# Two transformer layers at the end of a long kernel: weights awaited by halves, attention paced by one step per group, copies and stores rearranged

## The reference, cut to what matters

```
for l in range(DEPTH_2):                       # 2 layers
    proj = h @ w_in[l]                         # retention q,k,v,g; pool u; attention q,k,v; forget logits
    o_r  = silu(g_r) * head_group_norm(retention(q_r, k_r, v_r))      # 4 heads, width 384
    o_p  = multiscale_pool(u_p) * pool_scale                          # width 256
    o_f  = forgetting_attention(q_f, k_f, v_f, logf)                  # 6 heads, width 384, causal softmax
    h    = layer_norm(ALPHA * h + concat(o_r, o_p, o_f) @ w_out[l])
    h    = layer_norm(ALPHA * h + (silu(h @ w1[l]) * (h @ w3[l])) @ w2[l])    # D_FF = 2816
return h[:, 16:]
```

## Time and profile before

| | us |
|---|---|
| median of three runs | 3325.28 (3321.03 to 3330.27) |
| the profiled execution | 3315.55 |
| its span | 3313.3 |
| TensorE busy (matmul) in the span | 3153.7 (95%) |
| VectorE, ScalarE busy | 882.8, 555.3 |
| mean granted TensorE clock | 0.967 of full speed |

### The profile page before, as it was taken

The page is one execution under the profiler, slowest core; times in us unless marked ns, Lnnn a source line. Parts: engine busy times, 40 slices in busy tenths (PEclk is TensorE's granted clock), DMA queues, the critical chain, the costliest instruction groups (busy, mean ns, idle before and its releaser), DMA issues.

```text
span 3313.3 us, 52517 instructions
## 1 busy us (share of the span) xinstructions
PE 3153.7 (95%) x22815; PEld 1784.6 (54%) x22815; DVE 882.8 (27%) x1852; ACT 555.3 (17%) x1217; POOL 45.6 (1%) x58
## 2 busy tenths in 40 slices
PE   9878878999999999999989999999999999999998
PEld 3454545343434343434335667574785658675865
DVE  2633444212121211111263431323133112222101
ACT  1332310111111111111121310220112010120000
POOL 0000001000000000000010000000000000000000
PEclk9888878999999999999989999999999999999999
DMA  9800035999999999999843333323333353243531
GB/s 402 339 26 27 27 120 194 403 404 414 405 411 406 415 405 414 406 413 406 330 170 128 114 138 127 147 102 153 132 134 127 115 197 132 90 159 114 214 149 68
DMA packets 90266, 751.82 MB, mean 227 GB/s; under 512 B 9977, under 2 KB 24513, under 8 KB 50353
## 3 DMA queue, kind: packets, MB, share of 16 engines
q1 hardware_dynamic: 62080, 693.52, 52.8%
q10 hardware_dynamic: 21536, 30.51, 2.7%
q0 software_dynamic: 6544, 26.24, 2.1%
HBM read 683.10 MB, written 67.13 MB: 226 GB/s over the span
## 4 chain that ended last, share of the span: by engine, by line
PE 84%; DVE 3%; ACT 2%; DMA 1%; issue 1%; POOL 1%; ACTq 0%; POOLq 0%; DVEq 0%
PE psum L1207 20%; PE psum L1543 19%; PE psum L1284 10%; PE psum L1560 9%; PE psum L1487 5%; PE psum L1529 3%; PE psum L1498 3%; PE psum L772 3%; PE psum L1307 1%; PE psum L1160 1%; PE psum L790 1%; PE psum L1366 1%; PE psum L1404 1%; PE psum L1432 1%; PE psum L1377 1%
## 5 line engine op out<-in xcount | busy, mean ns | idle before, releaser
L1207 PE MATMUL psum<-weight_ring,arena 128*32 128x512 f32 x6192 | 691.4, 594 | 5.7 <-issue 5.4
L1543 PE MATMUL psum<-arena,weight_ring 128*128 128x256 f32 (+1 forms) x2816 | 632.7, 384 | 2.7 <-ACT arena L2169 2.7
L1543 PEld LDWEIGHTS psum<-arena,weight_ring 128*128 128x128 f32 x2816 | 528.9, 189 | 97.6 <-issue 10.4
L1207 PEld LDWEIGHTS psum<-weight_ring,arena 128*32 128x32 f32 x6192 | 197.2, 110 | 429.5 <-issue 416.7
L1284 PE MATMUL psum<-weight_ring,arena 128*32 128x256 f32 x6144 | 338.2, 380 | 1.0
L1560 PE MATMUL psum<-weight_ring 128*128 128x512 f32 x704 | 308.2, 597 | 4.2 <-DVE weight_ring L3069 4.2
L1284 PEld LDWEIGHTS psum<-weight_ring,arena 128*32 128x32 f32 x6144 | 196.6, 110 | 134.8 <-ACT arena L2049 8.6
L2807 DVE COPY arena<-psum 128x384 f32<-128x384 f32 x32 | 17.9, 559 | 802.8 <-PE psum L772 802.8
L1560 PEld LDWEIGHTS psum<-weight_ring 128*128 128x128 f32 x704 | 133.8, 191 | 171.9 <-issue 164.6
L1487 PE MATMUL psum<-weight_ring,arena 128*128 128x512 f32 (+2 forms) x512 | 171.8, 493 | 1.5 <-ACT arena L2169 1.5
L3069 DVE TENSOR_TENSOR weight_ring<-weight_ring,psum 128x256 f32<-128x256 f32 (+1 forms) x88 | 37.4, 425 | 501.8 <-PE psum L1543 498.5
(11 more groups left out here) (421 smaller groups left out, 2407.5 us busy)
## 6 DMA issues: line engine op xcount, KB each, us to landing
weight_ring<-exp_gu SPq DMA_DIRECT2D x129, 2048.0 KB, 13.3
weight_ring<-weights SPq DMA_DIRECT2D x104, 2048.0 KB, 7.8
weight_ring<-exp_down SPq DMA_DIRECT2D x64, 2048.0 KB, 12.8
x_sorted<-arena SPq DMA_DIRECT2D x2, 10752.0 KB
arena<-x_sorted ACTq DMA_DIRECT2D x33, 384.0 KB, 10.3
y_sorted<-arena ACTq DMA_DIRECT2D x128, 96.0 KB, 11.7
y_sorted<-arena SPq DMA_DIRECT2D x2, 5632.0 KB, 39.6
y_sorted<-arena SPq DMA_DIRECT2D x2, 5120.0 KB, 37.3
```

What stands on the lines that cost most here:

```text
L1207: mm = pe.matmul(psum[j * GROUP:(j + 1) * GROUP, g, :], xg[:, k, g * GROUP:(g + 1) * GROUP], w[:, kk, j * 512:(j + 1) * 512], start=(k == ...
L1543: mm = pe.matmul(bank[:, 0:b - a], w[:, k, col:col + P], h2_t[:, k, a:b], start=(k == 0), stop=(k == KT - 1))
```

## The change

- `mix` asks for the second W_OUT piece only when half 1 begins. It waits for the last softmax output only ahead of the last of the eight matmuls of the first group; before that it waits for the fourth of six units.
- The transposes of the retention rows and ScalarE's copies of them move from `mix` into attention step `turn_at = fox_at + 3`, in all four attentions. They use the ring `main` as before.
- `feed_down(1, A, 0)` takes one attention step per group, as all others do.
- Into the layers, ScalarE takes the last tile's two roots after its first and its third copy of turned rows, not ahead of all five. At the turn of (1, B) it takes the last root after its first copy.
- In `feed_down`, VectorE scales the tile before ahead of the wait for the group's matmuls, and makes the statistics of half 0 when half 0 is done.
- In layer 1 the scaled rows are written in two halves; SP, behind its last weight load, stores each half (256 KB) as it is ready. Pool stores nothing more.

The diff, without the parts that only pass arguments along:

```diff
@@ TensorE, attend @@
+                    if k == plan.turn_at:
+                        pe.wait_ge(sem("ret_ready"), run + 1)
+                        for t in rows_of(l, x):
+                            n = SIZE[t]
+                            bank = main.bank(pe)
+                            for e in range(3):
+                                mm = transpose(bank[:, e * n:(e + 1) * n], u2[0:n, t, U_QK + e * P:U_QK + (e + 1) * P], n)
+                            main.ship(mm, ("mix", l, t), "a")
@@ TensorE, mix @@
                 fox_turns.rest(pe)
-                pe.wait_ge(sem("ret_ready"), RUNS[l, x] + 1)
-                for t in rows_of(l, x):
...
-                pe.wait_ge(*job)
-                fox_outs.rest(pe)
-                ws = [weights(l, W_OUT + half) for half in range(2)]
+                pe.wait_ge(*main.drained_of(("mix", l, rows_of(l, x)[-1])))
+                pe.wait_ge(*fox_outs.drained_of(("fox", l, x, 3)))
+                ws = []
                 for half, t in rows_items(l, x):
+                    if t == WHOLE[x][0]:
+                        ws.append(weights(l, W_OUT + half))
...
                     for k in range(KT):
+                        if k == KT - 1 and (half, t) == (0, WHOLE[x][0]):
+                            fox_outs.rest(pe)
@@ all engines, layers @@
-                feed_down(1, "A", 0, steps, 2)
+                feed_down(1, "A", 0, steps)
@@ SP @@
-            sp.wait_ge(out_landed, 16 * TT)
+            for t in range(1, NT2):
+                for half in range(2):
+                    part = slice(half * 512, (half + 1) * 512)
+                    sp.wait_ge(sem("layer_start"), final_count(t, half))
+                    sp.dma_start(io["out"][(t - 1) * P:t * P, part], h2[:, t, part]).then_inc(out_landed, 16)
+            sp.wait_ge(out_landed, 16 * 2 * TT)
@@ Pool @@
-            for t in range(1, NT2):
-                pool.wait_ge(sem("layer_start"), start_count(LAYERS, t))
-                pool.dma_start(io["out"][(t - 1) * P:t * P, :], h2[:, t, :]).then_inc(out_landed, 16)
@@ ScalarE, gated_embedding @@
-                    rows_root(A, t)
-                    rows_root(A, t)
+                    if t + 1 < TT:
+                        rows_root(A, t)
+                        rows_root(A, t)
@@ ScalarE, attend: ahead of the copies and exponentials of the step @@
+                    if k == plan.turn_at:
+                        mix_rows(l, x)
@@ ScalarE, turn_rows: behind each copy @@
+                    if later:
+                        roots(later.pop(0))
@@ ScalarE, layers @@
-                project(0, "A", steps, EARLY_STEPS)
+                project(0, "A", steps, EARLY_STEPS, roots_after=(TT - 1, None, TT - 1))
-                feed_down(1, "A", 1, none)
-                turn_rows("mid", 1, "B")
+                last = feed_down(1, "A", 1, none, True)
+                turn_rows("mid", 1, "B", (last,))
@@ VectorE, norm_scaled @@
-                V.did(dve.scalar_tensor_tensor(row, row, deviation, ln_par2[0:n, 1, :], ALU.mult, ALU.add), ready)
+                for part in range(parts):
+                    cut = slice(part * D // parts, (part + 1) * D // parts)
+                    V.did(dve.scalar_tensor_tensor(row[:, cut], row[:, cut], deviation, ln_par2[0:n, 1, cut], ALU.mult, ALU.add), ready)
@@ VectorE, feed_down @@
+                centered, parts = None, 2 if l == LAYERS - 1 else 1
                 for half, t in rows_items(l, x):
-                    each(steps, n_steps)
+                    each(steps)
+                    if centered is not None:
+                        norm_scaled(centered, sem("layer_start"), parts)
+                        centered = None
                     bank = main.take(dve, ("down", l, c, half, t))
...
                     if c == 1:
-                        if centered is not None:
-                            norm_scaled(centered, sem("layer_start"))
-                            centered = None
-                        if half != 0:
-                            V.settle_other(main.drained["v"])
+                        V.settle_other(main.drained["v"])
+                        if half == 0:
+                            half_stats(t, 0)
+                        else:
                             dve.wait_ge(sem("layer_ln_landed"), 16 * landed)
                             centered = norm_centered(t)
```

More of the change, by code:

```diff
@@ L134, in __init__ @@
         self.units = [(m, u) for m in range(FH // 2) for u in range(2)]
+        self.turn_at = self.fox_at + 3
         self.steps = self.fox_at + len(self.units) + 2
@@ L688, in start_count, with final_count @@
             return t + 1 if l == 0 else NT2 + END_ORDER.index((l - 1, t)) + 1
+        def final_count(t, half):
+            return NT2 + len(END_ORDER) - len(rows_of(LAYERS - 1, "A")) - len(WHOLE["B"]) + 2 * (t - 1) + half + 1
         def project_items(x):
@@ L1545, in feed_up, with feed_down @@
                     piece_free[at] = main.done()
-            def feed_down(l, x, c, steps, n_steps=1):
+            def feed_down(l, x, c, steps):
                 a, b = span(l, x)
@@ L2170, in turn_rows, with project @@
                               main.drained["a"])
-            def project(l, x, steps=None, pace=(), items=(0, 99), mid_roots=()):
+                    if later:
+                        roots(later.pop(0))
+            def project(l, x, steps=None, pace=(), items=(0, 99), mid_roots=(), roots_after=()):
                 if items[0] == 0:
-                    turn_rows("start", l, x)
+                    turn_rows("start", l, x, roots_after)
                 roots(*mid_roots)
@@ L2214, in feed_up, with feed_down @@
                     A.did(act.activation(ff_t[:, f - FF_CHUNKS[c][0], 0:b - a], bank[:, 0:b - a], ACT.Silu), main.drained["a"])
-            def feed_down(l, x, c, steps, n_steps=1):
+            def feed_down(l, x, c, steps, leave=False):
                 last = None
                 for half, t in rows_items(l, x):
-                    each(steps, n_steps)
+                    each(steps)
                     if c == 1:
@@ L2222, in feed_down @@
                         last = t if half != 0 else None
-                if c == 1:
+                if c == 1 and not leave:
                     roots(last)
+                return last
             def feed(l, x, steps):
@@ L2247, in layers @@
                 each(steps, PLANS["B"].steps)
-                mix(0, "B")
                 roots(3)
@@ L2254, in layers @@
                 each(steps, PLANS["A"].steps)
-                mix(1, "A")
                 roots(1)
@@ L2260, in layers @@
                 feed_up(1, "A", 0, steps)
-                feed_down(1, "A", 0, steps, 2)
+                feed_down(1, "A", 0, steps)
                 feed_up(1, "A", 1, steps)
                 each(steps, PLANS["B"].steps)
-                mix(1, "B")
                 roots(3, 4)
-                feed_down(1, "A", 1, none)
-                turn_rows("mid", 1, "B")
+                last = feed_down(1, "A", 1, none, True)
+                turn_rows("mid", 1, "B", (last,))
                 feed(1, "B", none)
@@ L3069, in feed_up, with half_stats @@
                     V.did(dve.tensor_tensor(g, g, bank[:, 0:b - a], ALU.mult), main.drained["v"])
+            def half_stats(t, half):
+                n = SIZE[t]
+                V.did(dve.bn_stats(ln_stats[0:n, t, half * 6:half * 6 + 6], h2[0:n, t, half * 512:(half + 1) * 512]))
             def norm_centered(t):
@@ L3074, in norm_centered @@
                 row, stats = h2[0:n, t, :], ln_stats[0:n, t, :]
-                for half in range(2):
-                    V.did(dve.bn_stats(stats[:, half * 6:half * 6 + 6], row[:, half * 512:(half + 1) * 512]))
+                if t == 0:
+                    half_stats(t, 0)
+                half_stats(t, 1)
                 V.settle()
@@ L3142, in layers @@
                 feed_up(1, "A", 0, steps)
-                feed_down(1, "A", 0, steps, None, 2)
+                feed_down(1, "A", 0, steps)
                 feed_up(1, "A", 1, steps)
```

21 lines of the change are left out of this document (8 added, 13 removed).

## The result

The changed kernel takes 3277.66 us (median of 4 runs, 3277.50 to 3282.41), the kernel before in the same session 3324.86 us (4 runs, 3321.03 to 3330.27): ratio 0.986, interval 0.9843 to 0.9877. The gain is 47.2 us at the medians. A second session with 4 runs of the changed kernel and 23 of the one before gave 3282.10 against 3324.06, 42.0 us: ratio 0.9878, interval 0.9861 to 0.9896; that median lies inside the range.

The account below looks back on a forecast made before the run. TensorE bounds the kernel, so time moves only where it idles, runs at its lower clock, or the last DMA is awaited. Terms 14.3 + 3.4 + 7.8 + 4.8 + 2.3 = 32.6 us take 3325.28 to 3292.7 us, range 3279 to 3310.

Parts of the forecast that it names:

- the two largest terms: Weight waits at mix(0, B) and mix(1, A) with retention rows turned in attention, 14.3 us; one attention step per group, 7.8 us.
- hand-over into the layers: First projection after the first block: three of ScalarE's five copies ahead of the second root, gain 1.9 us (bounds 0.8, 3.0).
- tail: After the last matmul: less VectorE scaling and statistics, 2.0 us, smaller last store from SP, 0.3; sum 2.3 us.
- waits by halves, and turning: At the mixes: both weight waits (8.0, 7.9 us) go, retention-row transposes move into attention steps; 14.3 us gained.
- clock behind the two waits: mix(0, B) and mix(1, A) lose their lower-clock stretch after the weight stalls: 1.9 + 1.5 = 3.4 us.
- pace: feed_down(1, A, 0) and last attention: one step per group instead of two gains 7.8 us (bounds 4.6 and 9.5).
- turn in layer 1, and its clock: Between group B's down and up matmuls in layer 1: shorter gap 2.3 us, faster matmuls behind it 0.6.
- the rivals in which they return or stay: At the mixes: waits return for the norm's parameters (0.06), or stay because the first piece is late (0.03); 3312 us each.
- the small change (2.7 - 3.3 - 0.6 - 0.4): Turning and hand-overs: 2.7 us gone at unstalled mixes, less 3.3 transposes in steps, 0.6 new waits, 0.4 for four hand-overs.
- The second and third rivals: Last attention's paced steps: no cheaper through table switches, 3300.4 us (0.06); or each stalls in up groups, 3341.8 (0.04).
- The upper bound, 3.0: Hand-over into the layers: the most it could gain, 3.0 us, all of the wait before the first projection.
- a largest gain of 42.5: Whole kernel: all terms at their high ends, 16 + 5 + 9.5 + 7 + 5 = 42.5 us, giving 3282.8.

## Why the prediction was off

The direction held, and so did the mechanism of the two largest terms; the hand-over into the layers was misread, and the tail was priced without its queue. The size was 10.7 us short in the layers. Term by term, from the table of stretches and from the kernel with halves and turning alone, whose stretch from mix(1, A) to mix(1, B) takes 345.6 us (348.3 before, 338.5 after):

| term | forecast | measured | from |
|---|---|---|---|
| waits by halves, and turning | 14.3 | 16.1 | 0.1 + 7.7 + 7.4, 0.9 in the next stretch |
| clock behind the two waits | 3.4 | 5.4 | 2.0 + 1.8 + 1.6 |
| pace | 7.8 | 7.1 | 9.8 - 1.8 - 0.9, or 345.6 - 338.5 |
| hand-over into the layers | 1.9 | 5.3 | 10.72 - 5.43 |
| turn in layer 1, and its clock | 2.9 | 4.7 | 2.9 + 1.5 + 0.3 for mix(1, B) |
| tail | 2.3 | 4.7 | 11.99 - 7.32 |
| sum | 32.6 | 43.3 | |

**Weights by halves and turning (right for the pair, 1.8 short, wrong for each edit alone).** Waits of 8.0 and 7.9 us became none, and the rivals in which they return or stay fell: the norm's parameters (ln_mid, 11.5 us to landing after) hold up nothing. The prediction costed the two edits apart, though. It gave the turning 2.7 - 3.3 - 0.6 = -1.2 us and all of the 16 us to the halves. The sum came out, since it took for granted that both are made; for a reader who would make only one it was wrong. The exposed copies were priced at 1.10 + 0.44 by the earlier trace rows, the start of a mix ahead of which ScalarE has no root to wait for. At the two mixes in question the wait is 5.5 and 4.2 us. Which part of the small change (2.7 - 3.3 - 0.6 - 0.4) makes up the 1.8 us no run separates.

**The clock (short by 2.0).** The two mixes gained 2.0 and 1.8 us, about as forecast. Not forecast were 1.6 us at the down matmuls of feed_down(0, B), 22.48 us before and 20.87 after, behind a stall that both kernels have. The kernels with turning alone and with halves and turning have that gain, the ones with halves alone and with the pace alone have not: as far as eleven traces tell, it goes with the turning. It isn't sure to be had, though: in the kernel with whole tiles from SP the clock fell there again. Why turning changes the clock there no run shows.

**The pace (right, 7.1 to 7.7 us for 7.8).** The stall [4.59 <-DVE L3004] is gone. Over the last attention TensorE waits nowhere longer than 0.51 us. The chain of after from step 12 on, which answers to the earlier trace rows:
```profile
2838.40 10.50 PE psum L1570 x24
2849.32 10.33 PE psum L1570 x24
2860.51 20.60 PE psum L1570 x48
2881.11 6.91 PE psum L1553 x32
...
2960.12 14.01 PE psum L1553 x64
```
The last steps fall in up groups of 7.10 us, start to start 9.2 to 11.4 us apart; the difference is the steps' own matmuls, and no stall but three of 0.3 us for ScalarE's L2155. The second and third rivals predicted waits in these groups and fall with that. From step 12 (2836.85) to the mix it takes 137.3 us against 144.1, transposes of 0.7 us included.

**The hand-over (the step that failed most).** The prediction said that three copies lie ahead of the second root and two behind it. The diff has the root behind the loop over a whole tile's copies, so all five lie ahead. It was a misreading of one indentation, and the kernel with the order I had read gives 8.4 us where the real one gives 5.4: 3.0 of the 3.4 us that were missed. The upper bound, 3.0, came from the same reading and did not hold either.

**The turn in layer 1 (right, sizes short).** The gap is 3035.95 to 3039.05, 3.1 us, where it was 6.0: 2.9 us against 2.3. Behind it the 384 matmuls take 83.16 us, so all of the 1.5 us over the quiet rate came back, of which 0.6 was taken. After, at the turn, answering to the earlier trace rows:
```profile
3036.41 1.08 ACT L2185 COPY arena<-psum 128x512 f32<-128x512 f32 x2 [7.03 <-PE psum L777]
...
3037.74 0.29 ACT L1829 ACTIVATE arena<-arena 128x1 f32<-128x1 f32 x1 [0.26 <-DVE arena L3098]
...
3037.94 1.06 ACT L2185 COPY arena<-psum 128x512 f32<-128x512 f32 x2
...
3039.05 3.29 PE L1553 MATMUL psum<-arena,weight_ring 128*128 128x256 f32 x14 [1.10 <-ACT arena L2185]
```

**The tail (half right).** VectorE's part was 2.0 us in the forecast and is 1.8: from the last matmul to its last write 4.6 us in after, 6.4 before (writing in two halves took 0.13 us more, 1.42 for 1.29, where 0.05 was put). The store's part was 0.3 and is 2.9. It was priced by its size, from Pool's landing of 2.9 us in the earlier trace rows. It should have been priced by its queue as well, and from VectorE's last write to the end of the span instead of to the landing: of the 2.9 us, 2.0 lie behind the landing (2.4 against 0.4). The tail of after, answering to the earlier trace rows:
```profile
3268.47 0.69 DVE L3126 SCALAR_TENSOR_TENSOR arena<-arena,psum 128x512 f32<-128x512 f32 x1 [4.16 <-PE psum L1570]
3269.20 0.69 DVE L3088 BATCH_NORM_STATS2 arena<-arena 128x6 f32<-128x512 f32 x1
...
3270.17 1.29 DVE L3101 SCALAR_TENSOR_TENSOR arena<-arena 128x1024 f32<-128x1024 f32 x1
...
3271.57 1.42 DVE L3113 SCALAR_TENSOR_TENSOR arena<-arena 128x512 f32<-128x512 f32 x2
```
The Trainium skill (DMA: Bandwidth & Descriptors, section "Anatomy of one DMA — SWDGE (gpsimd) path") gave 0.6 us between 512 and 256 KB, an estimate from its 436 GB/s. The landings from SP agree at the median, 2.6 and 2.0; the last store itself, issued 0.66 us behind its other half, took 2.3. The same page (section "Specifications") puts the first byte at about 1 us for Pool's path and 0.6 for SP's, a rule that the prediction left out; 0.3 us between the two 512 KB landings are near it, the 2.5 us at the end of the span are not explained by it.

**From the profile to the median.** The prediction carried 32.6 us over to the median, on the ground that no term depends on which execution was profiled. The layers bear this out. But the total of one execution says little: the first block, which no edit touches, moves by up to 17.4 us from profile to profile. The gain by medians, 42.0 and 47.2 us in two sessions, has the layers' 43.1 to 44.4 between. The low end of the range rested on a largest gain of 42.5 and about 3.8 us for the spread. The layers' 43.2 alone would give 3325.28 - 43.2 = 3282.1, inside it; about 4 us more came from outside the layers in the first session and none in the second. So the terms are 10.7 us short by their own fault, and which side of 3279 the median fell on was chance. The step that failed most is the hand-over, 3.4 us of the 10.7; the tail (2.4), the clock (2.0), the turn in layer 1 (1.8) and the waits (1.8) follow, less 0.7 for the pace.

## What to carry to other kernels

When a long wait is taken away, look at what else ends just before it on every engine that feeds the waiting instruction. Whatever ends within the gain is the new wait, and two edits that remove one each, worth 3 to 4 us and at most 1 us apart, are worth 22 us together. Before a stall is priced from the chain, look in the timeline whether the engine stood: the chain went over VectorE for 4.0 us where TensorE had work for all but 0.34. Price an operation that moves by the work ahead of it in its engine's order at the new place, not by its duration at another place. Compare kernels stretch by stretch between landmarks of one profile; the total of a profiled execution mixes in parts that vary by themselves.

## What was not expected of the hardware

The end of the program after a last store: 2.4 us behind the landing when it is Pool's, 0.4 when it is SP's. The granted clock behind one and the same stall of 2.2 us was 1.00 in six traces and 0.51 to 0.63 in five, which costs 1.6 to 1.7 us each time. A longer stall doesn't mean a lower clock behind it, in one trace each: behind the 8.0 us gap of the kernel before it was 0.68 over 6 us, behind the 6.3 us gap of the kernel with halves alone 0.51:
```profile
2287.00:2293.00 6.00, 6.00 (x8) 2.48 (x9) 1.46 (x3) 0.00 (x0) 0.53 (x1) 0.51 0.99 423
```
